# Forgetting attention's queries and keys: projected with tokens on partitions, normed along the free axis, transposed back to heads

## The reference

```python
h = rmsnorm(x, norm_mix)
(fq, fk, fv, ff, gq, gk, gv, gb, ga, gz, sq, sk, sv, gates) = split_projection(h @ w_in)
fq = rmsnorm(heads(fq, 4), fox_qnorm)      # 4 heads of 128
fk = rmsnorm(heads(fk, 4), fox_knorm)
ya = fox_attention(fq, fk, heads(fv, 4), log_sigmoid(ff + fox_fbias))
```

## Time and profile before

| | |
|---|---|
| median of 3 runs | 1174.89 us (1174.74 to 1175.29) |
| the profiled execution's own time | 1173.07 us |
| its span in the trace | 1171.4 us |
| PE busy / weight loads | 1145.2 us (98%) / 999.7 us |
| DVE busy | 812.5 us (69%) |
| ACT busy | 622.3 us (53%) |
| GpSimd (POOL) busy | 82.1 us (7%) |

### The profile page before, as it was taken

How to read it: one execution, slowest core, us unless ns; L and a number is a source line. 1 busy time by engine, 2 the same in 40 slices (tenths; PEclk the granted TensorE clock), 3 DMA queues, 4 the chain that set the end, 5 groups by cost and what they waited for, 6 DMA issues and landing times.

```text
span 1171.4 us, 16802 instructions
## 1 busy us (share of the span) xinstructions
PE 1145.2 (98%) x6765; PEld 999.7 (85%) x6765; DVE 812.5 (69%) x881; ACT 622.3 (53%) x801; POOL 82.1 (7%) x114
## 2 busy tenths in 40 slices
PE   8999999999999999999999999999999998999997
PEld 7978898889987799999888888888777887888886
DVE  6897658756878568787548777547776747777743
ACT  7666446436478466565345444436456547444432
POOL 7101100200000000000000000002700000000000
PEclk9999999999999999999999999999999999999999
DMA  8654333334665354655655655555633534665560
GB/s 259 190 158 147 99 106 110 109 108 156 220 198 181 108 163 156 204 169 191 216 179 181 210 179 186 200 195 177 201 116 127 180 108 127 194 202 182 179 214 36
DMA packets 144420, 193.95 MB, mean 166 GB/s; under 512 B 6168, under 2 KB 121240, under 8 KB 144344
## 3 DMA queue, kind: packets, MB, share of 16 engines
q1 hardware_dynamic: 143144, 188.43, 49.7%
q0 software_dynamic: 1200, 4.46, 1.1%
HBM read 191.82 MB, written 1.05 MB: 165 GB/s over the span
## 4 chain that ended last, share of the span: by engine, by line
PE 83%; DVE 10%; ACT 4%; issue 2%; DMA 0%; DVEq 0%; ACTq 0%
PE banks L1328 23%; PE banks L1362 19%; PE banks L1310 13%; PE banks L1331 11%; DVE wlo L1920 4%; PE banks L1347 3%; PE banks L1338 2%; PE banks L1589 1%; PE banks L1477 1%; ACT whi L1649 1%; PE banks L1464 1%; PE banks L1376 1%; PE banks L1547 1%; DMA x_tok<-in_x 0%; DVE x_tok L2193 0%
## 5 line engine op out<-in xcount | busy, mean ns | idle before, releaser
L1920 DVE TENSOR_TENSOR wlo<-raw,whi 128x2048 fp32r<-128x2048 f32 (+1 forms) x178 | 406.5, 2291 | 122.5 <-ACT whi L1649 122.4
L1649 ACT ACTIVATE whi<-raw 128x2048 fp32r<-128x2048 f32 (+1 forms) x179 | 340.1, 1903 | 248.3 <-PE banks L1331 146.0
L1328 PE MATMUL banks<-xhl,whi 128*128 128x512 f32 x1232 | 396.2, 403 | 2.7 <-DVE y5l L2248 1.8
L1331 PEld LDWEIGHTS banks<-xhl,wlo 128*128 128x128 f32 x1232 | 231.4, 188 | 54.6
L1331 PE MATMUL banks<-xhl,wlo 128*128 128x256 f32 x1232 | 242.6, 278 | 0.0
L1328 PEld LDWEIGHTS banks<-xhl,whi 128*128 128x128 f32 x1232 | 188.9, 189 | 10.3 <-issue 5.6
L1310 PE MATMUL banks<-xhl,whi 128*128 128x256 f32 x912 | 165.5, 284 | 1.3 <-DVE xhl L1947 0.7
L1310 PEld LDWEIGHTS banks<-xhl,whi 128*128 128x128 f32 x912 | 142.0, 192 | 2.1 <-DVE xhl L1947 1.1
L1310 PE MATMUL banks<-xhl,wlo 128*128 128x256 f32 x456 | 129.0, 283 | 0.0
L1362 PE MATMUL banks<-whi,hh 128*128 128x512 f32 x264 | 102.9, 390 | 0.0
L1362 PE MATMUL banks<-wlo,hh 128*128 128x512 f32 x264 | 102.7, 389 | 0.0
(11 more groups left out here) (368 smaller groups left out, 1531.9 us busy)
## 6 DMA issues: line engine op xcount, KB each, us to landing
raw<-in_w_in SPq DMA_DIRECT2D x40, 1024.0 KB, 5.3
raw<-in_w_up SPq DMA_DIRECT2D x22, 1024.0 KB, 5.8
raw<-in_ffn_w_gate SPq DMA_DIRECT2D x22, 1024.0 KB, 5.3
raw<-in_ffn_w_up SPq DMA_DIRECT2D x22, 1024.0 KB, 5.3
raw<-in_ffn_w_down SPq DMA_DIRECT2D x22, 1024.0 KB, 5.0
raw<-in_w_down SPq DMA_DIRECT2D x11, 1024.0 KB, 5.6
raw<-in_w_out SPq DMA_DIRECT2D x8, 1024.0 KB, 5.2
raw<-in_xa_wkv SPq DMA_DIRECT2D x8, 1024.0 KB, 5.7
```

Of the source, the lines that this page charges most:

```text
L1328: pe.matmul(bank(b[m]), wh[:, k, m * P:(m + 1) * P], both[:, k, :, :].rearrange("p a t -> p (a t)"), start=(k == 0), stop=(k == KD - 1), s ...
L1331: ins = pe.matmul(bank(b[m])[:, 0:T], wl[:, k, m * P:(m + 1) * P], Xh[:, k, :], start=False, stop=(k == KD - 1), skip_group_check=True)
L1649: act.activation(columns(whi, c, part), columns(raw, c, part), ACT.Copy).then_inc(act_done, 1)
L1920: dve.tensor_tensor(columns(wlo, c, part), columns(raw, c, part), columns(whi, c, part), ALU.subtract).then_inc(dve_done, 1)
```

## The change

The queries' and keys' four chunks become kind V. ACT copies them out in token layout into the same memory (`by_token`). Then, per tensor: ACT squares both token halves (`tn_sq`), DVE reduces them along the free axis to eight sums a partition (`tn_red`), ACT makes the roots (`tn_r`), DVE multiplies with the roots broadcast over 128 elements (`tn_mul`), PE transposes eight 128x128 blocks into banks 6 and 7 (`tn_t`), and ACT copies them out into `fq_` or `fk_` with the gain as scale (`tn_e`). The sums by ones, their roots over 512 elements and the multiplies of fq and fk go. The planner gets durations and inputs for the new steps; the waits on `hn_mul` of `fk1` become waits on `tn_e` of `fk`.

```diff
@@ -70,7 +70,7 @@
 
 ROUGH = {"lo": 2.29, "hi": 1.92, "add": 1.23, "copy": 1.2, "cv_mul": 0.9, "cv_add": 2.2, "cv_silu": 0.63, "gated": 1.35,
          "ns": 1.06, "nr": 0.42, "nd": 0.66, "nh": 0.95, "nl": 0.48, "resid": 1.22, "gsig": 4.6, "gzs": 4.0, "tables": 1.5,
-         "hn_sum": 0.86, "hn_sq": 0.63, "hn_r": 1.3, "hn_mul": 0.75,
+         "tn_sq": 1.26, "tn_red": 1.4, "tn_r": 0.5, "tn_mul": 1.35, "tn_t": 0.88, "tn_e": 1.26, "hn_sum": 0.86, "hn_sq": 0.63, "hn_r": 1.3, "hn_mul": 0.75,
          "rows0": 0.41, "rows0p": 1.3, "rows1": 1.3, "rows2": 2.4, "rows3": 3.4, "rows3b": 2.0, "rows4": 0.9, "rows5": 0.42, "rows6": 0.5,
          "rows7": 0.7, "heads_apart": 2.2,
          "g_dec": 0.86, "g_mask": 1.3, "g_exp": 1.25, "g_kk": 1.8, "g_m": 2.4, "g_turn": 1.8, "g_kb": 2.0,
@@ -183,8 +183,7 @@
     out.append(dict(kind="S", srcs=[((0, 8), kpn(w[win][:, GB:GB + 8])), ((8, 12), kpn(w[win][:, FF:FF + 4])),
                                     ((12, P), kpn(w[win][:, GZ:GZ + P - 12]))], x="x", banks=(2,), evac="rows"))
     for what, c0 in (("fq", FQ), ("fk", FK)):
-        for i in range(2):
-            wide(win, c0 + 256 * i, "x", "add", to=what, i=i)
+        vals(win, c0, "x", "vcopy", to=what)
     vals(win, FV, "x", "vcopy", to="fv")
     for what, c0 in (("sq", SQ), ("sk", SK)):
         for i in range(2):
@@ -280,12 +279,15 @@
             return pl.ended.get(("copy", max(c for c, ch in enumerate(chunks) if ch.get("to") == "mv")), 1e9)
         if name == "sc" and args[0] == "mem" or name == "pt" and args == ["mem", 0]:
             return pl.ended.get(("hn_mul", "mq1" if name == "pt" else f"mq{args[1] // 2}"), 1e9)
+        if name == "tn_t":
+            return pl.ended.get(("hn_mul", "gk1"), 1e9)
         if name == "rows0p":
             return pl.ended.get(("rows0",), 1e9)
         if name == "g_dec":
             return pl.ended.get(("heads_apart",), 1e9)
         to, i = {"hn_sq": (str(args[0])[:2], int(str(args[0])[2:] or 0)) if name == "hn_sq" else None,
                  "sc": {"moba": ("qk", 2 + args[1] // 4), "xa": ("xq", args[1])}.get(args[0]) if name == "sc" else None,
+                 "tn_sq": (args[0], None) if name == "tn_sq" else None,
                  "pv": ({"moba": "bv", "fox": "fv", "mem": "mv", "xa": "xv1"}[args[0]], None) if name == "pv" else None,
                  "z_s": ("sk", 1), "z_o": ("sv", None)}.get(name) or (None, None)
         for c, ch in enumerate(chunks):
@@ -590,6 +592,11 @@
                          + [("act", "hn_sq", after) for after in jobs[n + 1:n + 2]])
         return links
 
+    def token_norm(m):
+
+        return [[("act", "tn_sq", m), ("dve", "tn_red", m), ("act", "tn_r", m)], [("dve", "tn_mul", m)],
+                [("pe", "tn_t", m), ("act", "tn_e", m)]]
+
     def gdn(t):
         c = [[("pe", "g_dec", t), ("dve", "g_mask", t), ("act", "g_exp", t)],
              [("pe", "g_kk", t), ("dve", "g_m", t)],
@@ -651,7 +658,7 @@
     for _ in range(4):
         mm(c)
         c += 1
-    b += hn("fq0", "fq1", "fk0", "fk1")
+    b += token_norm("fq") + token_norm("fk")
     side.append(b)
     mm(c)
     mm(c + 1)
@@ -839,6 +846,7 @@
         fbias, alog, dtb, ealog = (small[0:4, 36 + i:37 + i] for i in range(4))
         per_gate = small[0:4, 36:39]
         gsc = small[:, 40:41]
+        token_root = small[:, 8:16]
         nmx = [small[:, 42:44], small[:, 44:46]]
         rsm = [small[:, 46:48], small[:, 48:50]]
         rrc = [small[:, 50:52], small[:, 52:54]]
@@ -1046,7 +1054,11 @@
         NORM = {"norm_mix": (x, xh, xl), "norm_xq": (x, xh, xl), "norm_ffn": (x, xh, xl), "norm_mem": (memx, mh, ml),
                 "ffn1_pre_g_2": (x, xh, xl), "mix_pre_g_2": (x, xh, xl), "xa_pre_g_2": (x, xh, xl),
                 "ffn2_pre_g_2": (x, xh, xl), "mem_g_2": (memx, m2h, m2l)}
-        TO = {"fq": fq_, "fk": fk_, "sq": sq_, "sk": sk_, "mk": mk_, "mq": mq_, "qk": qk_, "xk": xk_, "xq": qk_,
+        def by_token(t):
+
+            return t[:, :, :].rearrange("p h t -> p (h t)").rearrange("p (a b) -> p a b", a=NT)
+
+        TO = {"fq": by_token(fq_), "fk": by_token(fk_), "sq": sq_, "sk": sk_, "mk": mk_, "mq": mq_, "qk": qk_, "xk": xk_, "xq": qk_,
               "pin": pin, "gz": gz_, "gate": gates, "fv": fv_, "sv": sv_, "mv": mv_, "bv": bv_, "xv0": xv_[:, :, 0:512], "xv1": xv_[:, :, 512:1024]}
 
         def pcolumn(name, i=0):
@@ -1059,14 +1071,12 @@
             HN[f"gq{i}"] = (gq_[:, s, :], gKb, gVb, 7, None, 1.0, float(HD) ** -0.5, None)
             HN[f"gk{i}"] = (gk_[:, s, :], gKb, gVb, 7, None, 1.0, 1.0, None)
             HN[f"go{i}"] = (gq_[:, s, :], gKb, gVb, 4, pcolumn("gdn_onorm"), 1.0 / HD, 1.0, gz_[:, s, :])
-            HN[f"fq{i}"] = (fq_[:, s, :], S1, PT1, 6, gsc, 1.0 / HD, 1.0, None)
-            HN[f"fk{i}"] = (fk_[:, s, :], S1, PT1, 6, pcolumn("fox_knorm"), 1.0 / HD, 1.0, None)
             HN[f"mq{i}"] = (mq_[:, s, :], xv_[:, 0, 0:512], xv_[:, 0, 512:D], 5, pcolumn("mq_norm"), 1.0 / HD, 1.0, None)
             HN[f"mk{i}"] = (mk_[:, s, :], S2[0], PT2[0], 4, pcolumn("mk_norm"), 1.0 / HD, 1.0, None)
 
 
         HN_BEFORE = {}
-        for jobs in (("gq0", "gk0", "gq1", "gk1", "go0", "go1"), ("fq0", "fq1", "fk0", "fk1"), ("mk0", "mk1", "mq0", "mq1")):
+        for jobs in (("gq0", "gk0", "gq1", "gk1", "go0", "go1"), ("mk0", "mk1", "mq0", "mq1")):
             HN_BEFORE |= dict(zip(jobs[1:], jobs))
 
 
@@ -1421,6 +1431,19 @@
                 pe.matmul(bank(b), ones[:, :], flat(sq[:]), start=True, stop=True).then_inc(pe_done, 1)
 
 
+            def tn_t(m):
+
+                pe.wait_ge(dve_done, at("tn_mul", m))
+                if m == "fq":
+                    pe.wait_ge(dve_done, at("hn_mul", "gk1"))
+                else:
+                    pe.wait_ge(act_done, at("tn_e", "fq"))
+                src = TO[m]
+                for t in range(NT):
+                    for h in range(NH):
+                        ins = pe.transpose(bank(6 + t)[:, h * P:(h + 1) * P], src[:, t, h * P:(h + 1) * P], ident[:, :])
+                ins.then_inc(pe_done, 1)
+
             def g_dec(t):
                 pe.wait_ge(dve_done, at("rows7"))
                 pe.wait_ge(pool_done, at("consts2"))
@@ -1519,8 +1542,7 @@
                     if kind != "fox":
                         pe.wait_ge(dve_done, at("ol", kind, p))
                 if kind == "fox":
-                    pe.wait_ge(dve_done, at("hn_mul", "fk1"))
-                    pe.wait_ge(dve_done, at("hn_mul", "gk1"))
+                    pe.wait_ge(act_done, at("tn_e", "fk"))
                     pe.wait_ge(dve_done, at("heads_apart"))
                 elif kind == "mem":
                     pe.wait_ge(dve_done, at("hn_mul", f"mq{h // 2}"))
@@ -1757,6 +1779,28 @@
                 link(act.activation(flat(rr[:]), bank(b), ACT.Ln, bias=eps, scale=inv))
                 act.activation(flat(rr[:]), flat(rr[:]), ACT.Exp, scale=-0.5).then_inc(act_done, 1)
 
+            def tn_sq(m):
+
+                act.wait_ge(act_done, at("copy", chunk_of(m, None)))
+                if m == "fk":
+                    act.wait_ge(dve_done, at("tn_red", "fq"))
+                act.activation(S1[:, :], TO[m][:, 0, :], ACT.Square)
+                act.activation(PT1[:, :], TO[m][:, 1, :], ACT.Square).then_inc(act_done, 1)
+
+            def tn_r(m):
+                act.wait_ge(dve_done, at("tn_red", m))
+                link(act.activation(token_root, token_root, ACT.Ln, bias=eps, scale=1.0 / HD))
+                act.activation(token_root, token_root, ACT.Exp, scale=-0.5).then_inc(act_done, 1)
+
+            def tn_e(m):
+
+                act.wait_ge(pe_done, at("tn_t", m))
+                act.wait_ge(dve_done, at("params_c"))
+                gain = gsc if m == "fq" else pcolumn("fox_knorm")
+                for t in range(NT):
+                    ins = act.activation((fq_ if m == "fq" else fk_)[:, :, t * P:(t + 1) * P], per_head(bank(6 + t)), ACT.Copy, scale=gain)
+                ins.then_inc(act_done, 1)
+
             def g_exp(t):
                 act.wait_ge(dve_done, at("g_mask", t))
                 act.activation(gM[:, :, :], gM[:, :, :], ACT.Exp)
@@ -1845,7 +1889,7 @@
             def yh(br):
 
                 act.wait_ge(pe_done, at("z_o", NH - 1))
-                act.wait_ge(dve_done, at("hn_mul", "fk1"))
+                act.wait_ge(act_done, at("tn_e", "fk"))
                 if br == 1:
                     act.wait_ge(dve_done, at("hn_mul", "go1"))
                 act.activation(ybh[br][:, :, :], (fq_, gq_, sq_)[br][:, :, :], ACT.Copy).then_inc(act_done, 1)
@@ -2014,6 +2058,19 @@
                     if s < 3:
                         link(ins)
                 ins.then_inc(dve_done, 1)
+
+            def tn_red(m):
+                dve.wait_ge(act_done, at("tn_sq", m))
+                if m == "fk":
+                    dve.wait_ge(dve_done, at("tn_mul", "fq"))
+                dve.tensor_reduce(token_root[:, 0:4], per_head(S1[:, :]), AX_X, ALU.add)
```

(7 more changed lines are left out.)

## The result

The changed kernel takes 1182.12 us (median of 4 runs, 1180.52 to 1182.99) against 1174.85 us for the kernel before (1174.74 to 1175.29). The ratio is 1.006, with a 95% interval of 1.0044 to 1.0076: slower by some 7 us, where 2.5 us less were forecast, and outside the range. The profiled execution took 1182.07 us.

The account below looks back on a forecast made before the run. PE, busy 98% of the 1171.4 us span, was taken as the bound. Its work at -2.24 us and the order at -0.25 summed to -2.5 us: 1172.4 us against the median, range 1170.6 to 1175.6.

Parts of the forecast that it names:

- PE's work, -2.24 us: Query and key chunks on PE: transposes add 1.75 us, sums by ones save 3.51, the projection saves 0.48.
- DVE -4 us, ACT +0.7 us, hidden: Query and key norms: DVE relieved by 4 us, ACT loaded by 0.7, both hidden under PE but for two waits.
- The price of a transpose in the Trainium skill: About 275 ns per transpose on PE; 16 at full price cost 4.4 us instead of 1.75, making the sum +0.4.
- The order of the work: Links behind the change move, dealing the stage's 1.86 us of PE idle time anew: -0.25 us, bounds -1.9 to +1.9.
- (a): PE's work goes, but one or two new waits take back 0.5 to 1.5 us: 1173.0 to 1174.1; chance 0.3.
- What would show it: Signs in the trace: stage near 223.2 us if right; long transposes, low-part waits or new waits elsewhere if wrong.
- some room for an order that is worse than any row shows: Part of the 0.12 chance of slower by over 0.2%, above 1177.2 us, beside 0.09 for DVE delaying the low part.
- (c): DVE meets the norms' reduction early and delays a later chunk's low part: up to +6.1 us, 1181.0; chance 0.1.

Follow-up runs that it names:

- e5: The changed kernel in the order of the kernel before, with the keys' multiply placed a quarter of a chunk earlier: 1171.87 us, ratio 0.998.
- e9: e5 with the turn of gk_ and gv_, the last stick-breaking head and the last delta rule norm placed later: 1172.80 us.
- e10: The kernel before with the turn of gk_ and gv_, the last stick-breaking head and the last delta rule norm placed later: 1175.40 us.
- e2: The kernel before, in the order that the planner wrote for the changed kernel: 1187.41 us, ratio 1.0123.
- e3: The changed kernel with the planner's margin in the stage lowered from 0.5 us (0.6 for the delta rule) to 0.3: 1175.53 us.
- e4: The kernel before with the planner's margin in the stage lowered from 0.5 us (0.6 for the delta rule) to 0.3: 1180.31 us.
- e6: e5 with each of the 16 transposes done twice into the same place: 1172.73 us, ratio 0.9985.
- e8: The changed kernel with its own planner and the margin lowered to 0.4 us for both chains: 1178.76 us, ratio 1.0034.
- e1: The changed kernel in the order that the planner wrote for the kernel before: 1173.84 us, ratio 0.9997.
- e11: e5 with the turn of gk_ and gv_ and the last delta rule norm placed a quarter of a chunk later: 1170.08 us.
- e12: The changed kernel in its own planner's order, with each of the 16 transposes done twice: 1183.61 us, ratio 1.0083.
- e7: The changed kernel, its planner's DVE clock charged 1.23 us per chunk for the removed adds, in the books only: 1177.82 us, ratio 1.0036.

## Why the prediction was wrong

- **PE's work, -2.24 us**: right in kind, near in size. Its parts measured 0.87 us a group of transposes, and the sums are gone. In pairs of the same order the medians differ by 2.5 (e5 and before, but for e5's one moved multiply), 2.6 (e9, e10) and 5.3 us (changed, e2; on two chips), and the stages without waits by 1.8, 2.3 and 1.5. The last pair differs more in the whole because norms by ones meet waits of their own in that order (1.94 and 1.76 us in e2). e3 and e4 are no such pair, as the planner wrote each its own order with the margin of 0.3: e3's longest wait in the stage, 1.95 us at 170.85, is before an `l_x`, e4's, 2.50 us at 206.65, before a link of stick-breaking. They differ by 4.8 us, the stages without waits by 1.5, too; behind the 2.5 us wait that both have before the first output projection, only e4 has a stretch at half clock. That the forecast's -2.5 us and e5's agree is partly luck: the work is nearer to -1.8 than to -2.24 us in the stage.
- **DVE -4 us, ACT +0.7 us, hidden**: the prices were near. Reductions 0.68 against 0.61 (a pair takes 1.28), multiplies 1.22 against 1.23, gain copies 0.69 against 0.59. But DVE did not get 4 us: it is busy for 162.22 us in the changed stage against 162.63, and 160.56 in e5. Of its old steps, the 27 low parts take 63.1 us against 62.0, the four scalings of `z_lk` 3.4 against 2.4, and the longest low part (3.36 us, at 103.29) and the scaling at 211.49 ran beside POOL's masks. The earlier trace rows had a sign of this that the prediction took for a price: its 1.273 us is the mean of two multiplies of fk_, 0.75 us at 110.43 and 1.79 us at 105.24, the second beside POOL's masks (101.89 to 106.49). ACT's busy time grew by 0.1 us (116.84 to 116.94). A group of transposes costs 0.87 us in the changed kernel, as in the earlier trace rows, and 0.88 in e6. The price of a transpose in the Trainium skill (TensorE: Matmul & The Clock Gate, Part 4: PE-mode transpose), which would have given +0.4 us, does not hold here as time on PE.
- **The order of the work** is the step that failed. It said that the 1.86 us of idle time would be dealt anew, by -1.9 to +1.9 us, and that the planner is not meant to leave PE a wait for the new steps' inputs. The bound was taken from the total of one order, which said nothing of what another one deals: five waits and 1.8 us became fourteen and 9.5. And a margin of 0.5 or 0.6 us is a wait that the planner accepts, on books that leave POOL's masks out: `ROUGH` has 1.3 us for `z_lk`, which takes 2.45 in the rows above (210.90 to 213.35). Nor does `fits` look at what a link's later steps put in front of another chain's on DVE.
- **The rivals.** (a) named the right mechanism, waits that come back, and in "What would show it" even the place, the delta rule and the stick-breaking heads; but at a price of up to 1.5 us instead of 9. What came had 0.03 of the chances, "some room for an order that is worse than any row shows". (c) named DVE in front of the low part; no wait of PE in the stage ends in a low part. The sign was wrong because I asked what the new steps do to their neighbours, and not what a planner that is fed new numbers does to links 80 us away. What stood in the code: every later link is placed against clocks that the change moves.
- That the kernel before was a favourable draw could hardly be seen in its trace alone. Of the six orders that the planner wrote for either data path (before 0.5 and 0.3; changed 0.5, 0.4, 0.3 and charged), its is the fastest: the other five take 1.1 (e3) to 7.3 us more (changed), whichever the data path.

What stays open: why the changed kernel's stage is left with 222.0 us and e8's with 221.9 without waits, where e1, e3, e5 and e11 have 220.8 to 221.2. Small gaps below a tenth of a microsecond behind interrupted chunks may sum to it; it was not measured. Open too is which property of an order brings the waits: packing doesn't settle it (e8), and no run took one of the meetings behind 180 us apart by itself.

## What to carry to other kernels

Where an automatic order stands between the code and the engines, price a change in two runs: one with the order held, which shows what the operations are worth, and one with it free. The waits of one order give no bound for those of the next. A link that gives PE a quarter of a chunk to cover a chain over ACT and DVE is safe only while no other chain is put in front of it on those queues.

## What the runs showed of the hardware

- Behind PE's waits of 1.97 us (e1), 1.95 us (e3 and e8) and 2.50 us (e4) the granted clock fell from 1.00 to about half, the level of 1.2 GHz, for some 3 us, 1.7 us each; behind those of 1.8 us in e9 and e10, and behind the fourteen shorter ones of the changed kernel, it did not. The length of one wait doesn't decide alone: in e2 the clock stayed at 1.00 behind 1.94 us (before 98.88) and fell behind 1.76 us (before 112.25). Nor do the same wait and the same code: PE waits 2.2 us for `y2l` near 400 us in every kernel, and behind it the clock fell in the traces of the changed kernel (0.56 at 406 us), e5 and e6, and stayed at 1.00 in those of before, e9 and e11; the 2.5 us wait before the first output projection was followed by a fall in e4 (0.50 from 296 to 298 us) and by none in e3. Single runs of one kernel lie in groups 1.7 us apart (e9: 1171.0, 1172.7, 1174.4 us), as if the number of such stretches varied between executions. The traces fit that: those of the changed kernel, e5, e6 and e12 with one near 400 us are of runs 1.5 to 1.7 us above the fastest of their kernel, those of e7, e9 and e11 without one are within 0.2 us of the fastest.
- Some DVE operations and POOL's masks shut each other out. Beside the masks a multiply over 1024 elements took 2.29 instead of 1.22 us (e1), a scaling over 384 took 1.33 instead of 0.36, and a low part 3.38 instead of 2.28 (e5); the first two end 1.1 and 0.2 us behind POOL's mask. Not so the reductions out of the banks: that of sq_ in e1 (103.11) took its 1.22 us beside the masks. In return the pair of masks, begun 0.1 to 0.2 us behind a low part or a multiply, takes 4.6 (before, e1) to 5.6 us (e5), where one alone takes 1.3 (206.12 in the kernel before). The Trainium skill (SBUF — State Buffer, Who interferes with whom) says that the pair of SBUF ports that the two share is an exclusive lock held for a whole instruction, not a split of bandwidth; the trace agrees for these operations, and by it any of them can be late by up to one mask.
- Eight fp32 transposes cost PE 0.87 us and eight more 0.88 us, though each record lasts 272 ns.
